# Weight halves moved by 64 bytes in a two-model decoder kernel of split float32 products

## What is computed

```python
x = x + concat([y_ssm, y_att]) @ w_out
x = x + memory_attention(rmsnorm(x), rmsnorm(mem), w_mq, w_mk, w_mv, w_mo)
x = x + (silu(gate) * val) @ w_down      # gate, val = causal_dwconv(h @ w_up)
...
q, k, v = split(modulate(rmsnorm(x)) @ w_qkv)
x = x + gate_a * (attend(q, k, v, k_c, v_c, bias) @ w_o)
x = x + gate_f * ffn(modulate(rmsnorm(x)))
```

## Time and profile before

| what | value |
|---|---|
| median of 3 runs | 4233.17 us (4232.87 to 4234.36) |
| the profiled execution's own time | 4234.58 us |
| its span | 4232.5 us |
| TensorE matmuls busy | 3871.9 us, 91% |
| weight loads busy | 3116.3 us, 74% |
| VectorE busy | 2306.1 us, 54% |
| ScalarE busy | 1706.0 us, 40% |
| GpSimd busy | 1576.0 us, 37% |
| TensorE in the chain that ended last | 79% of the span |
| mean granted TensorE clock | 0.959 of full speed |

### The profile page before, as it was taken

The page is one execution under the profiler, slowest core; times in us unless marked ns, Lnnn a source line. Parts: engine busy times, 40 slices in busy tenths (PEclk is TensorE's granted clock), DMA queues, the critical chain, the costliest instruction groups (busy, mean ns, idle before and its releaser), DMA issues.

```text
span 4232.5 us, 57565 instructions
## 1 busy us (share of the span) xinstructions
PE 3871.9 (91%) x19930; PEld 3116.3 (74%) x19930; DVE 2306.1 (54%) x3140; ACT 1706.0 (40%) x2662; POOL 1576.0 (37%) x830
## 2 busy tenths in 40 slices
PE   6998799999989997998999889999999978899999
PEld 5865577788768665777887677778877976667877
DVE  2578741467534787424675675644235757663234
ACT  3543333333335443333333532654334543463333
POOL 3401353455344013544553413133553143204553
PEclk9999799999999997999999899999999999999999
DMA  3210132355222100323553232213222532002222
GB/s 112 94 55 30 35 105 90 113 175 180 94 80 90 60 30 30 105 95 105 174 180 107 82 103 75 81 56 110 94 92 98 179 121 73 26 11 85 94 89 90
DMA packets 107739, 391.15 MB, mean 92 GB/s; under 512 B 11952, under 2 KB 12080, under 8 KB 107184
## 3 DMA queue, kind: packets, MB, share of 16 engines
q1 hardware_dynamic: 88704, 321.95, 22.6%
q10 hardware_dynamic: 16416, 57.62, 4.0%
q0 software_dynamic: 2448, 9.24, 0.6%
HBM read 386.67 MB, written 2.10 MB: 92 GB/s over the span
## 4 chain that ended last, share of the span: by engine, by line
PE 79%; DVE 11%; ACT 3%; issue 3%; POOL 3%; DMA 0%; ACTq 0%; DVEq 0%; POOLq 0%
PE ps L529 20%; PE ps L531 19%; PE ps L530 19%; PE ps L685 2%; PE ps L1791 2%; POOL arena_parts L497 2%; PE ps L864 2%; PE ps L707 2%; PE ps L1801 2%; DVE conv L431 2%; PE ps L376 1%; PE ps L1819 1%; ACT arena_parts L489 1%; DVE rstd L394 1%; PE ps L1512 1%
## 5 line engine op out<-in xcount | busy, mean ns | idle before, releaser
L497 POOL TENSOR_TENSOR arena_parts<-ring,arena_parts 128x1024 fp32r<-128x1024 f32 x490 | 1178.4, 2405 | 1898.2 <-ACT arena_parts L489 1695.7
L530 PE MATMUL ps<-arena_parts 128*128 128x512 f32 (+1 forms) x3256 | 1225.3, 376 | 0.0
L489 ACT ACTIVATE arena_parts<-ring 128x1024 fp32r<-128x1024 f32 x580 | 612.9, 1058 | 1511.1 <-PE ps L531 1420.7
L529 PE MATMUL ps<-h_parts,arena_parts 128*128 128x512 f32 x2256 | 901.9, 400 | 53.1 <-issue 32.5
L531 PE MATMUL ps<-h_parts,arena_parts 128*128 128x512 f32 x2256 | 884.5, 392 | 0.0
L1315 DVE SCALAR_TENSOR_TENSOR conv<-ps,cols,conv 128x511 f32<-128x511 f32 (+3 forms) x536 | 377.7, 705 | 683.8 <-ACT conv L1326 475.3
L530 PEld LDWEIGHTS ps<-arena_parts 128*128 128x128 f32 x3256 | 626.8, 192 | 107.3 <-issue 2.6
L529 PEld LDWEIGHTS ps<-h_parts,arena_parts 128*128 128x128 f32 x2256 | 427.1, 189 | 164.2 <-issue 40.8
L531 PEld LDWEIGHTS ps<-h_parts,arena_parts 128*128 128x128 f32 x2256 | 427.2, 189 | 91.2
L529 PE MATMUL ps<-quarters_parts,arena_parts 128*128 128x512 f32 (+1 forms) x880 | 335.0, 381 | 57.2 <-issue 33.9
L1401 DVE TENSOR_TENSOR arena_parts<-arena,quarters_parts 128x1024 fp32r<-128x1024 f32 x88 | 216.4, 2462 | 227.7 <-ACT quarters_parts L1395 227.7
(11 more groups left out here) (259 smaller groups left out, 6258.4 us busy)
## 6 DMA issues: line engine op xcount, KB each, us to landing
ring<-in_stream SPq DMA_DIRECT2D x612, 512.0 KB, 3.3
ctx<-in_mod ACTq DMA_DIRECT2D x48, 512.0 KB, 3.3
sq<-in_mod ACTq DMA_DIRECT2D x48, 512.0 KB, 3.3
sq<-in_bias POOLq DMA_DIRECT2D x8, 512.0 KB, 4.7
conv<-in_bias POOLq DMA_DIRECT2D x8, 512.0 KB, 4.5
arena<-in_mem ACTq DMA_DIRECT2D x2, 1024.0 KB, 4.7
out_y<-x ACTq DMA_DIRECT2D x8, 256.0 KB, 2.7
x<-in_x SPq DMA_DIRECT2D x4, 256.0 KB, 4.8
```

What stands on the lines that cost most here:

```text
L489: act.activation(w_high[:, t % 2, :], ring[:, t % RING, :], ACT.Copy).then_inc(S["h_ready"], 1)
L497: eng.tensor_tensor(w_rest[:, t % 2, :], ring[:, t % RING, :], w_high[:, t % 2, :].bitcast(F32), ALU.subtract)\
L529: pe.matmul(out, w_h, x_h, start=start, stop=False)
L530: pe.matmul(out, w_h, x_r, start=False, stop=False)
```

## The change

The arena is 16 elements (64 bytes a partition) longer. `w_high`, `w_rest` and `na_probT` lie 16 elements further on, and so do `tcols` and, by way of the arena's end, `last512`. All that is allocated after the arena moves on by 64 bytes too. All other cuts of the arena, and the buffers before it, stay where they are. No instruction and no semaphore is added, taken away or reordered.

```diff
-        ARENA = 23040
+        ARENA = 23056
         arena = sb("arena", [P, ARENA])
...
-        w_high, w_rest = cut_parts(18432, 2, TILE), cut_parts(20480, 2, TILE)
+        w_high, w_rest = cut_parts(18432 + 16, 2, TILE), cut_parts(20480 + 16, 2, TILE)
...
-        tcols = cut(22528, 3, 4 * 16)
+        tcols = cut(22544, 3, 4 * 16)
...
-        na_probT = [cut(20480 + 1024 * s, 1024) for s in range(2)]
+        na_probT = [cut(20496 + 1024 * s, 1024) for s in range(2)]
```

## The result

The changed kernel takes 4286.84 us (4280.75 to 4288.06, four runs) against 4233.13 us, a ratio of 1.0123 with a 95% interval of 1.0109 to 1.0137. The forecast of no change was wrong, and so was its range: 53.7 us more, 6.8 above the upper end.

A forecast was written before the change was run, and what follows sets the result against it. The period of TensorE's split matmuls was taken to bound the kernel (matmuls busy 91%). Stationary reads 0, moving reads +1 us and other engines 0, from the median of 4233.17, gave 4234 us; range 4198 to 4280.

The forecast's parts named there:

- the threshold of 0.6 ns a matmul: Split matmuls on TensorE: smallest period change that a measurement could tell from no change, 8.5 us over 13,680 matmuls.
- the surplus of 13.3 ns over the columns: Split matmuls: period beyond column time at both 512 and 256 columns, 182 us in all, what addresses could move.
- the price of the stationary reads: Weight loads of the split matmuls, 13,056 of 13,680, from blocks shifted by 64 bytes: claimed to cost 0.
- the bounds of +6.7 and -10.3 ns: Limits per split matmul for shifted stationary reads: +91 us if two memory units become three, -141 us if a clash ends.
- The vT rows: Latent attention's plain-form value block loads (L707) at odd multiples of 256 bytes, 0.111 us each: claimed straddling costs nothing.
- The argument from slack: Weight loads at 512 columns: repeated every 0.120 us at 256, so at least 107 ns of slack within the 0.227 period.
- One more unit: Rival, split matmuls: shifted block touches one more memory unit; +46 us (4279) at 128 bytes, +91 (4324) at 256; chance 0.21.
- Clash removed: Rival, split matmuls: stationary and moving reads no longer meet; whole -141 us (4092), a quarter -35 us (4198); chance 0.15.
- The moving operands' 1 us: L635 to L637, weight halves as moving operand, 624 matmuls leaving the 2048-byte grid: 6 and 2 us possible, 1 taken.
- The halves' 0: Writes of w_high and w_rest (L489, L497) on other engines: 5 us if 5% slower, 0 taken.
- the side moves' 0: Short 128-column reads of the moved probabilities and identity: 0 taken, with 2 us as bound.
- the bound of two units, 4324: Upper limit for split matmuls: with 256-byte memory units two become three, +6.7 ns each, +91 us.

The follow-up runs named there:

- the streams: Kernels of matmul streams alone, 48 matmuls per operand placement, nothing else running; fp32r at 512 columns: 0.2269 us a matmul on the grid, 0.2333 with the load 64 bytes on.
- The bfloat16 streams: Matmul streams alone at 512 columns in bfloat16 instead of fp32r, load and stream 0 to 192 bytes apart: 0.2156 to 0.2160 us a matmul.
- the three products: Streams alone of high x high, high x rest, rest x high in the kernel's order; 256 columns, both weight halves 64 bytes on: 0.1135 us, against 0.120 all on one place.
- the two versions made from it: Kernel before with half buffers 4352 bytes apart, halves moved 64 bytes only in 256-column products: 4229.04 us; or in all products but those: 4285.74 us.

## Why the prediction was wrong

- **What bounds the kernel, the counts and the periods** were right. 13,680 matmuls one behind the other turned 6 ns into 54 us, and the threshold of 0.6 ns a matmul was sound. So was the place to look at: the surplus of 13.3 ns over the columns.
- **The step that failed** is the price of the stationary reads, "I take 0, since the 256-byte and 512-byte steps, the nearest rows, both show 0". Those rows are true and say nothing of the change: the pattern repeats every 256 bytes, so all of them are the same phase, and 64 is another. The step measured +6.3 ns at 512 columns and -2 to -6 at 256 (-2.8 on average), within the bounds of +6.7 and -10.3 ns that were written down; the sum took 0.
- The vT rows were of the plain form, and the streams show that form blind to the distance (41.36 us both). They could not stand for fp32r.
- "A constant surplus at every phase looks like the form's own cost" was half right: bfloat16 and plain float32 haven't got it. But its size depends on the distance, and on the width too: the same 13.3 ns at 512 and at 256 columns, on which the text leant twice, is a coincidence of these two widths (16.9 at 480).
- The argument from slack, that a load with 107 ns to spare can't show, failed too: the period moved by more at 512 columns, where the slack is, than at 256.
- **The rivals.** "One more unit" gave 46 us and came nearest in time, by another mechanism: both operands 64 bytes on cost nothing. Its sign, 0.233 in the wide rows, did show, and so couldn't tell the two apart; the 0.114 at 256 columns could. "Clash removed" had the mechanism in part, the distance between the two reads, and the wrong sign at 512 columns: the common phase, which it took for the clash, is the best placement there; at 256 columns it had the right sign. That narrow and wide products could go opposite ways was no case of the prediction.
- The moving operands' 1 us was right: 480 x 2.5 ns. The halves' 0 was right, and the side moves' 0 as well.
- Of the two rules of the Trainium skill that were weighed, "TensorE: Matmul & The Clock Gate", section "Back-to-back issue gap", gives N/2.4 + 2.5 ns, about 216 at 512 columns. The bfloat16 streams agree (0.2156 to 0.2160), fp32r doesn't (0.2267 at best). The section calls this the gap of an isolated matmul and gives about 131 ns for a stream of loads and matmuls at 512 columns; no stream of that width here has less than 0.2156. "SBUF — State Buffer", section "Who interferes with whom", gives the moving operand and the load ports of their own. By that the sum was to be 0, and the trace disagrees for fp32r: the period depends on the distance of the two reads, and the kernel took 54 us more. Whether they meet at a port or elsewhere isn't shown.
- The range ended at one unit of 128 bytes, 4280, although the bound of two units, 4324, was written down. That was too narrow for what the text knew: the only fine step that mattered was in no row, and the chance of 0.60 for no change stood on rows of another form and another phase.

## What to carry to other kernels

Keep stationary and moving operands of fp32r matmuls at a common place modulo 256 bytes when the moving operand has 512 columns; a buffer that slips by 32 or 64 bytes costs 3% of each such matmul at the full clock, silently. For other widths try 0, 64, 128 and 192 in a kernel of streams alone, one source line for each, and with the products in the kernel's order: at 256 columns one stream gave 0.1177 for a distance of 64 and the three products 0.1135. Don't expect the sum to the microsecond: the two versions made from it came out 4 to 14 us off. And rows that agree with one another are evidence only for what they vary: ask which phase, form and width they share with each other but not with the change.

## What the runs showed of the hardware that was not expected

- The fp32r matmul of 512 columns at the 2.4 GHz level has a period of 0.2267 us at distance 0, 0.2333 at 64, and comes back at 256; with both operands moved by the same 64 bytes it doesn't change. In the changed kernel, at distance 64, short and long periods alternate, whatever the line.
- At 256 columns distance 0 is among the dearest placements (0.120 against 0.1135).
- Fewer stationary columns make it no cheaper at distance 0: 0.2300 with 96, 0.2317 with 32.
- The surplus over the columns isn't the same at all widths: 13.3 ns at 512, 16.9 at 480, 11.9 at 288.
- bfloat16 (0.2156 to 0.2160) and plain float32 (41.36 us for 96, at both distances) don't depend on it.
